# A two-block transformer kernel on one core: fillers, front, halved weight splits, MLP banks and the layer norms' row scaling changed

## The reference, cut to what matters

```python
def _layernorm(x, g, b):
    mu = jnp.mean(x, -1, keepdims=True); var = jnp.mean(jnp.square(x - mu), -1, keepdims=True)
    return (x - mu) * lax.rsqrt(var + LN_EPS) * g + b
def first_block(x, ...):
    for i in range(2):
        h = _multiscale_pool(x, pool_w, pool_scale) if i == 0 else _diff_attention(x, ...)
        x = _layernorm(ALPHA * x + h, ln_mix_g[i], ln_mix_b[i])
        x = _layernorm(ALPHA * x + _swiglu(x, ...), ln_ffn_g[i], ln_ffn_b[i])
def second_block(x, ...):
    x = x + token_mixer(rms_norm(x, norm_mix_g), ...)
    x = x + squared_relu_mlp(rms_norm(x, norm_mlp_g), w_up, w_down)
    return rms_norm(x, final_norm_g)
```

## Time and profile before

| | us |
|---|---|
| median of 3 runs (997.61 to 999.0) | 998.71 |
| profiled execution | 998.4 |
| its span, first to last instruction | 996.2 |
| PE busy | 977.4 (98%) |
| DVE busy | 665.5 (67%) |
| ACT busy | 449.8 (45%) |
| DMA, mean | 177 GB/s |

### The profile page before, as it was taken

The page is one execution under the profiler, slowest core; times in us unless marked ns, Lnnn a source line. Parts: engine busy times, 40 slices in busy tenths (PEclk is TensorE's granted clock), DMA queues, the critical chain, the costliest instruction groups (busy, mean ns, idle before and its releaser), DMA issues.

```text
span 996.2 us, 15345 instructions
## 1 busy us (share of the span) xinstructions
PE 977.4 (98%) x6071; PEld 863.7 (87%) x6071; DVE 665.5 (67%) x814; ACT 449.8 (45%) x562; POOL 32.4 (3%) x54
## 2 busy tenths in 40 slices
PE   8999999999999999999999999999999999999997
PEld 7888888888996888888889878899999888888886
DVE  3776767685776876666676477775876656666663
ACT  3444444445665253434334446565654443434342
POOL 1000001000001000000001000000000000000000
PEclk9999999999999999999999999999999999999999
DMA  9756677548532456656543644543565535656541
GB/s 307 233 185 228 190 238 220 193 147 226 157 128 85 148 192 231 206 194 195 184 146 136 193 143 127 158 128 127 170 212 178 194 135 171 207 176 207 170 168 43
DMA packets 142175, 176.20 MB, mean 177 GB/s; under 512 B 7040, under 2 KB 120898, under 8 KB 142126
## 3 DMA queue, kind: packets, MB, share of 16 engines
q1 hardware_dynamic: 139040, 167.07, 52.1%
q0 software_dynamic: 2464, 8.30, 2.8%
q10 hardware_dynamic: 622, 0.14, 0.1%
HBM read 174.40 MB, written 1.09 MB: 176 GB/s over the span
## 4 chain that ended last, share of the span: by engine, by line
PE 88%; DVE 5%; ACT 3%; issue 2%; DMA 1%; ACTq 1%; POOL 0%; DVEq 0%; POOLq 0%; SPq 0%
PE bank L499 87%; DVE w_lo L990 2%; ACT w_hi L982 1%; PE bank L634 1%; PE bank L742 1%; DMA raw<-w_up 1%; DVE arena L1430 1%; DVE x_both L1360 0%; POOL rstd L1885 0%; ACTq L1250 0%; ACT bank L1258 0%; DVE arena L1455 0%; DVE arena L1444 0%; ACT arena L1139 0%; ACTq L1253 0%
## 5 line engine op out<-in xcount | busy, mean ns | idle before, releaser
L990 DVE TENSOR_TENSOR w_lo<-raw,w_hi 128x2048 fp32r<-128x2048 f32 (+1 forms) x157 | 353.5, 2256 | 164.2 <-ACT w_hi L982 164.0
L499 PE MATMUL bank<-x_both,w_hi 128*128 128x256 f32 (+1 forms) x2128 | 439.3, 330 | 2.6 <-DVE arena L1430 1.4
L499 PEld LDWEIGHTS bank<-x_both,w_hi 128*128 128x128 f32 x2128 | 357.6, 189 | 44.3 <-issue 6.7
L982 ACT ACTIVATE w_hi<-raw 128x2048 fp32r<-128x2048 f32 (+1 forms) x157 | 294.9, 1881 | 109.6 <-PE bank L499 98.7
L499 PE MATMUL bank<-x_both,w_lo 128*128 128x256 f32 x1520 | 287.6, 283 | 0.4 <-DVE arena L1430 0.4
L499 PEld LDWEIGHTS bank<-x_both,w_lo 128*128 128x128 f32 x1520 | 230.2, 191 | 3.9 <-issue 0.6
L499 PE MATMUL bank<-w_hi,arena_r 128*128 128x512 f32 x608 | 172.5, 392 | 1.2 <-DVE arena_r L1463 1.0
L499 PEld LDWEIGHTS bank<-w_hi,arena_r 128*128 128x128 f32 x608 | 113.1, 188 | 25.6 <-issue 2.4
L499 PE MATMUL bank<-w_lo,arena_r 128*128 128x512 f32 x304 | 96.1, 391 | 0.0
L1430 DVE TENSOR_REDUCE arena<-bank 128x512 f32<-128x1024 f32 x57 | 69.7, 1222 | 24.8 <-PE bank L499 24.8
L499 PE MATMUL bank<-w_hi,x_both 128*128 128x512 f32 x256 | 75.0, 393 | 2.3 <-DVE x_both L1360 0.8
(11 more groups left out here) (155 smaller groups left out, 612.2 us busy)
## 6 DMA issues: line engine op xcount, KB each, us to landing
raw<-w_up SPq DMA_DIRECT2D x76, 512.0 KB, 4.6
raw<-w_down SPq DMA_DIRECT2D x76, 512.0 KB, 4.3
raw<-w_in SPq DMA_DIRECT2D x60, 512.0 KB, 4.5
raw<-w_gate SPq DMA_DIRECT2D x44, 512.0 KB, 4.8
raw<-w_qkv SPq DMA_DIRECT2D x24, 512.0 KB, 5.0
raw<-w_o SPq DMA_DIRECT2D x16, 512.0 KB, 4.4
table<-bias_vectors POOLq DMA_DIRECT2D x12, 256.0 KB, 4.9
raw<-w_pa SPq DMA_DIRECT2D x4, 512.0 KB, 4.2
```

The source lines that it names most:

```text
L499: return nc.tensor.matmul(*a, skip_group_check=True, **k)
L982: last = nc.scalar.activation(o, i, ACT.Copy)
L990: last = nc.vector.tensor_tensor(o, i, h.bitcast(F32), ALU.subtract)
```

## The change

**Halved splits.** A unit other than the narrow one (`U_KI`) is rounded and split in two halves of 1024 columns. `hi_done` counts halves, so VectorE can begin when the first half is rounded.

**Layer norms 0, 1 and 3.** VectorE only centres and multiplies by the gain; ScalarE multiplies the rows by the root in place (L1078 after). The offset vector stands as two rows (minus its high part, minus its rest) and TensorE adds it in PSUM with matmuls of two contraction rows ahead of the transposes, which then accumulate. The rows in `x` get their offset later (`v_natural`, four VectorE instructions, L1492 after), where the seeds of the next sum need them. In norm 4 VectorE multiplies by the RMS gain and ScalarE by the RMS root. The order of x_lo pieces in norms 0, 3 and 4 changes too.

**Fillers.** 45 in place of 126: norm 0 has 1 and 3, norm 1 none, norm 3 has 1 and 3, norm 4 has 12 ahead, 12 and 3, norm 5 has 7 and 3.

**Front.** The pooling scale comes as one row on ScalarE's queue and TensorE spreads it to all partitions through PSUM; norm 0's gain and offset are loaded ahead of the first weight unit; the three small matmuls stand ahead of the mixing; PSUM is opened by four matmuls.

**MLP banks.** The up-projection of chunk 1 uses banks 6 and 7 and does not wait for VectorE.

```diff
 def rest_unit(eng, unit, slot, indexer=False):
-            eng.wait_ge(hi_done, unit + 1)
+            for h in range(0 if indexer else 2):
+                eng.wait_ge(hi_done, unit * 2 + (h + 1))
+                c = slice(h * UW // 2, (h + 1) * UW // 2)
+                last = nc.vector.tensor_tensor(w_lo[slot][:, c], raw[slot][:, c], w_hi[slot][:, c].bitcast(F32),
+                                               ALU.subtract)
...
+        def pe_offsets(eng, ev, quarters):
+            eng.wait_ge(off_ready, LAYER_NORMS.index(ev) + 1)
+            for i, h in quarters:
+                b = quarter(ev, i, h)[1]
+                for k in range(4):
+                    mm(b[:, k * P:(k + 1) * P], off[:, (4 * h + k) * P:(4 * h + k + 1) * P], minus_ones,
+                       start=(k == 0), stop=False)
 def pe_norm_end(eng, ev, src, idle, rounds):
-            pe_norm(eng, ev, src, ((0, 0), (0, 1)))
+            for h in range(2):
+                if ev in LAYER_NORMS:
+                    pe_offsets(eng, ev, ((0, h),))
+                pe_norm(eng, ev, src, ((0, h),))
             keep_warm(bank[5], idle)
+            if ev in LAYER_NORMS:
+                pe_offsets(eng, ev, ((1, 0), (1, 1)))
             pe_norm(eng, ev, src, ((1, 0), (1, 1)))
             eng.wait_ge(x_ready, 4 * rounds + 1)
-            keep_warm(bank[4], 5)
+            keep_warm(bank[4], 3)
...
+        def s_scale(eng, ev, i):
+            eng.wait_ge(rstd_ready, ROOT_OF[ev] + i)
+            for h in range(2):
+                eng.wait_ge(c_ready, 4 * LAYER_NORMS.index(ev) + 2 * i + h + 1)
+                nc.scalar.activation(x[:, i, half(h)], x[:, i, half(h)], ACT.Identity,
+                                     scale=rstd[:, i:i + 1]).then_inc(n_ready, 1)
...
-            s_rounds(eng, 0)
+            s_offsets(eng, ln0_in, 32)
+            s_split(eng, 0)
+            for i in range(NT):
+                s_scale(eng, 0, i)
+                s_rounds(eng, 0, (i,))
             s_split(eng, 1)
             s_ffn(eng, 0)
...
             v_split(eng, u0 + 3)
+            for i in range(NT):
+                v_natural(eng, (0, 3)[f], i)
             silu(0)
...
-            pe_norm_end(eng, 3, x, 24, 3)
+            pe_norm_end(eng, 3, x, 1, 3)
             pe_ffn(eng, 1, 3)
-            keep_warm(bank[5], 30)
-            pe_norm_end(eng, 4, nbuf, 14, 4)
+            keep_warm(bank[5], 12)
+            pe_norm_end(eng, 4, nbuf, 12, 4)
...
-            pe_norm_end(eng, 5, nbuf, 16, 6)
+            pe_norm_end(eng, 5, nbuf, 7, 6)
...
-            load_ffn(eng, 0, load_ln0)
+            load_ln0()
+            load_ffn(eng, 0)
...
+                if fresh:
+                    project_apart(slot, pair67).then_inc(unit_done, 1)
+                    return
                 eng.wait_ge(up2_read, i)
```

228 lines of the change are left out of this document (163 added, 65 removed).

## The result

The changed kernel took 988.6 us in the median (987.21 to 990.21, 4 runs), the kernel before 998.73 beside it: a ratio of 0.9903, 95% interval 0.9886 to 0.992. The forecast was 987, range 983.5 to 992.5. The four runs are 990.21, 989.85, 987.34 and 987.21: two pairs 2.7 us apart, which no part of the forecast spoke of. The profiled execution took 990.21, its span is 988.4; it belongs to the upper pair.

What follows compares the result with a forecast made beforehand. TensorE, busy 98% of the span, bounds the kernel; gains lie in needless work or waits, mainly at norms. Terms summed to -11.85 us on a median of 998.71, giving 987, with 8 in 10 within 983.5 to 992.5.

Steps and rivals of the forecast that it cites:

- the prediction's own signs of being wrong: Listed: TensorE waiting for busy ScalarE, gap over 1.5 us before second up-projection, first projection behind 27.5, window 0.9 or less at a norm.
- front to 58.37: Front and first feed-forward: mixing ends at 21.0, first projection at 26.0 for 29.64, part given back; -2.4 us.
- ends of both feed-forwards: Halved splits let the rest end earlier, shortening the gap at 206.03 and its twin; together -0.9 us.
- norm 1: ScalarE splits a whole unit between tile 0's scalings and roundings, so the projection starts at 217.0 instead of 216.55; +0.45 us.
- norm 3: Fillers run too long and scaling on VectorE go; projection starts at 339.15 instead of 342.38; -3.2 us.
- norm 4: Fewer fillers ahead and scaling on ScalarE; first projection at 535.9 for 538.88; -3.0 us.
- mixer and gates: Halved splits add VectorE work where it is nearly full in the mixer; +0.3 us, bounds -0.5 to +2.
- norm 5: With 7 fillers for 16, transposes follow VectorE's rows; projection at 809.4 for 811.12; -1.7 us.
- MLP banks: The wait of 1.41 for banks 4 and 5 at 818.34 goes, as chunk 1 uses others; -1.4 us.
- The rival of the clock: With fillers gone the clock drops in norms 0, 3, 4 and 5, 5.8 us each, ending at 1010; chance 0.04.
- ScalarE as the norms' bound: Scalings or roundings behind one more whole split in norms 0, 1, 3, 4 give 7.6 us back: 994; chance 0.16.
- The halves cost what they add: 0.16 us a unit reaches TensorE in mixer and gates, so 6 us come back: 993; chance 0.09.

Runs made afterwards that it cites:

- banks_old: Changed kernel with the MLP's second up-projection back in banks 4 and 5, which VectorE must read first; 989.04 us, ratio 0.9907.
- best_n3: The run best with norm 3 back on VectorE as in the kernel before, but 15 fillers behind tile 0 instead of 24; 984.59 us, ratio 0.9872.
- front_dma: Changed kernel with the pool scale by broadcast DMA and PSUM opened by 16 plain warm matmuls, as in the kernel before; 987.2 us, ratio 0.9887.
- n1_old: Changed kernel with norm 1 as in the kernel before: VectorE scales and adds the offset, no offset matmuls, 6 fillers; 986.47 us, ratio 0.9878.
- best: Changed kernel with the edits of front_fill and n1_old together; 984.18 us, ratio 0.9871.
- fillers_only: Kernel before with only the numbers of fillers set as in the changed kernel; 996.11 us, ratio 0.9965.
- front_fill: front_dma with three more fillers around the small matmuls, one ahead and two behind; 986.64 us, ratio 0.9881.
- whole_splits: Changed kernel with each weight unit split in one 2048-wide instruction on ScalarE and one on VectorE, as before; 994.11 us, ratio 0.9956.
- spread_full: Changed kernel with the scale spread by matmuls of 128 contraction rows instead of one; 987.67 us, ratio 0.9894.

## Why the prediction was right, step by step

The time fell into the range, 1.6 us above the forecast of 987. That it came so near is in part luck: the halved splits gave about 5 us more than they were put at, and the front (in its late form 3.3) and norm 1 (2.4) gave back about as much. Two of the prediction's own signs of being wrong are there in the profile of the changed kernel: a first projection behind 27.5 (30.82), and windows at 0.9 or less at a norm (0.84 and 0.82 at norm 1). Profiled execution against profiled execution, each term as the difference between the same instructions:

| term | forecast | measured |
|---|---|---|
| front to 58.37 | -2.4 | +0.9 (late form), -2.9 (early, banks_old) |
| ends of both feed-forwards | -0.9 | -1.6 |
| norm 1 | +0.45 | +2.9, +1.3 with a full clock |
| heads and O norm | none | -0.8 |
| norm 3 | -3.2 | -2.4 |
| norm 4 | -3.0 | -2.7 |
| mixer and gates | +0.3 | -1.2 |
| norm 5 | -1.7 | -1.6 |
| MLP banks | -1.4 | -1.6 |
| rest, with the tail | 0 | +0.3 |
| sum of the span | -11.85 | -7.8 (late form) |

**Halved splits: mis-sized.** The step "in the bulk of the kernel I take nothing for it" failed, and "-0.9 + 0.3" with it: the runs give -5.5. The forecast asked where TensorE waits for a rest and priced two gaps, at 206.03 and its twin at 517.75, with 0.9; they gave 1.6. It left out the gaps at 318.19, 643.98 and 782.67, which gave 2.0 (heads 0.8, mixer and gates 1.2): each is ended by a VectorE instruction other than a rest, and the profile of before had them, beside the 164.0 us of VectorE waiting for ScalarE ahead of its splits. Part of the 5.5 is inside the terms of the front and of norm 4, so the table's rows without the halving would be worse by that much. The Trainium skill ("VectorE: DVE Perf Modes", the section on the TRN2 errata) was weighed against the halving for its fixed cost per instruction. That cost is there, 0.15 and 0.19 us a unit by the durations, but the page asks only for tiles of 512 elements or more, which halves of 1024 still are, so the prediction read more against halving into it than it says.

**Front: right in one form, wrong in the other.** "It ends at 21.0" came out as 21.18 in the early form; the chain behind it took 5.9 us instead of 4.95 in both. That the early form is ahead of the forecast at 58.37 all the same (-2.9 for -2.4) is because nothing was given back: from the first projection to that matmul banks_old takes 28.42 us (28.73 before), where 30.0 were forecast, and the gap at 47.01 is 0.36 and not about 1.0. In the late form the mixing ends at 24.94. The step that failed there is the assumption that all front matmuls run at the full rate; the forecast had the small matmuls but gave the spread, its one-row matmuls and the copies it waits for no place ahead of the pooling.

**The chain of norm 3** was put at 4.95 from the end of the last matmul and is 5.8 (336.33 to 342.13). Offsets and transposes of tile 0 are four groups of 0.59 us each, where 0.45 and 0.5 were forecast, and end 2.35 us behind the last matmul instead of 1.74; all that follows is late by this 0.6, and the last steps add the rest. On the offsets, the Trainium skill ("TensorE: Matmul & The Clock Gate", "LDWEIGHTS") has it that a weight load goes by columns and not by rows. The trace agrees: the changed kernel's weight loads of two rows take 185 ns in the mean, those of its fillers with 128 rows 192, both 128 columns wide. The split into causes was wrong as well: half of the gain was put down to VectorE's scaling, and best_n3 shows 0.4.

**Norm 1** failed by what it left out. "ScalarE now splits a whole unit between" was not the cost; the offset matmuls are. Sixteen of them stand on TensorE's own path, where before it ran 6 fillers: 1.3 us (front_dma's rows, and gone in n1_old). The rest, 1.6, is the clock.

**The rival of the clock** was half right. It said norms 0, 3, 4 and 5, at 5.8 us each, with idle as the cause. What came was norm 1, at 1.6 us (2.8 in banks_old), with no idle in TensorE's row ahead. Over all fourteen profiles: with offsets and transposes ahead of the projection the clock fell in norm 1 in 4 of 9 and in norm 3 in 5 of 11; with fillers or plain transposes there it fell in norm 1 in 0 of 5, and in norm 3 in 0 of 2 with 15 or 24 fillers; in norm 0 it fell in best and in fillers_only, in norm 4 in fillers_only. Counts this small go with the offsets as a cause but don't show it. The Trainium skill (the same page, "HAM oscillation") ties a falling clock to waits in which TensorE is idle; that fits fillers_only (2.92 us of idle in norm 3), and not norm 1 of the changed kernel, where the row is busy throughout.

**ScalarE as the norms' bound** did not come true in the changed kernel: no wait of TensorE at its norms is for a scaling or rounding that stood behind a split (in norm 4 it waits twice 0.56 us for a scaling, but that one waited for GpSimd's root). It does come in norm 0 once the front is early (0.71 in front_fill). **The halves cost what they add** is refuted by whole_splits. Norms 4 and 5 and the MLP banks came out within 0.3. Norm 4 was measured as a whole only; how much of it is fillers and how much the scaling on ScalarE has no run (fillers_only gained 0.35 there, with a fallen clock).

Left open: what decides between the two forms of the front, since the same code shows both, and whether it is the matmuls of one and two rows that bring the clock down; spread_full was meant to tell, and its one profile is too little.

## What to carry to other kernels

Go through every gap of the bounding engine, also the ones ended by an instruction that the edit doesn't touch: what stands ahead of that instruction in its engine's list can be what the edit makes shorter. Here the forecast looked for waits for a rest and priced two gaps of 0.48 us; 66 us less waiting in VectorE's list were worth 5.5 us, through gaps of 0.33 to 0.59 us that other VectorE instructions ended. A filler that ends when the wait ends costs nothing, and in best_n3's profile 15 of them held the clock; count them against the row they cover: 9 of 24 too many were 2 us in norm 3, and with one alone the clock fell and took 1.25 of these 2 back. Moving work to the bounding engine to relieve another pays only in the stages where that engine stands idle: offset matmuls with scaling on ScalarE were worth 0.4 us in norm 3 and cost 1.3 in norm 1.
